# A two-layer decoder on eight cores: instruction order planned for transposes that land late, half of the second layer's weights cast while loading, casts and weight loads in smaller rows

## The chip, the cores and the metric

The program runs on the 8 cores of one Trainium2 chip, each core on one sequence of the batch. A core has five engines that follow their own instruction lists and meet through semaphores: TensorE (PE, matrix products into PSUM), VectorE (DVE), ScalarE (ACT), GpSimd (POOL) and SyncE (SP, which here only issues DMAs). POOL issues DMAs too; those are the only ones that change the number type on the way. The time is device microseconds of the slowest core.

## The reference

```python
x = _mlstm_layer(x, ...)                   # layer A
kv = einsum("bsd,de->bse", x, kv_w)        # shared keys and values
x = _stick_breaking_layer(x, k, v, ...)    # layer B

# layer A
u = einsum("bsd,de->bse", x, w_in)         # q,k | v | o | z | gates
qk = silu(causal_depthwise_conv(qk))       # width 4
h = mlstm_chunkwise(q, k, v, i, f)         # 8 heads; state carried from chunk to chunk
h = sigmoid(o) * head_norm(h) * silu(z)
x = layernorm(ALPHA * x + h @ w_out)
# layer B, 16 heads
q, z = split(x @ w_in)
A[t,s] = sigmoid(z_ts) * prod_{s<j<t}(1 - sigmoid(z_tj)), s < t
x = layernorm(ALPHA * x + (A @ v * silu(z)) @ w_out)
```

Width 2048, sequence 2048, all in float32 outside; the kernel multiplies in bfloat16.

## The kernel before

**How the program is made.** Each part of the work is a generator ("stream") that yields `Op` objects and conditions. `Sched.run` takes, again and again, the stream whose next operation could start earliest by a model of the engines, and records it. So the model decides in which order each engine's list stands; at run time each engine follows its list strictly and waits where an operand is not there. `KB.est` gives the start: the engine's own time, and for each operand the modelled end of its last writer and readers. For a DMA, `KB.dma` models one shared transfer clock `tdma`, to which each transfer adds its `cost`, and says that all it reads and writes is free 1.2 us after that (L157). This holds for what a DMA reads as well: its source may be overwritten only then.

**Layer A, head by head** (8 heads, 32 weight tiles w of two halves u):

- `aload` (L388) has POOL load each weight half from `a_wu` in float32 into RW as bfloat16, 512 KB per DMA; RW holds three w. `wsum` (L439) makes sums and differences of quarters of w, five operations of 1024 columns (L449), three on DVE and two on POOL. They are the stationary operands of a Strassen-like product of `grp` (L586): seven products of eight matmuls each (L604), 56 matmuls for each of 60 groups, 3360 in all; `st["slot"]` counts its steps, seven per group, some 420 in all. `gev` (L614) takes them out of PSUM with ACT (L622) and DVE (L637, L650, L664).
- `conv` (L698) does the convolution and SiLU of q and k for a stretch tb of 512 positions; its last step is on POOL (L723). For k, SP then issues a transpose from KTa (in REGX) to KN (in REGH): "REGH<-REGX". `vtr` (L732) transposes v from VTa (REGH) to VN (REGW): "REGW<-REGH".
- The recurrence has 16 blocks of 128 positions per head, written (head, block). `knw` scales KN on ACT (L779), `recf` is the first matmul of a block (L790, with the mask on DVE at L793), `recm` the others (L804, L806, L810) and the state (DVE L818, ACT L823). `reco` normalises: DVE L836 to L846, POOL L844, and ACT L849, which frees the PSUM bank that L790 of the second block after it writes. The result is transposed by SP ("REGW<-REGW", `hbt`), multiplied by the gates on DVE (L865, `htg`) and stored in `mida`.
- The first block of each stretch tb, that is, blocks 0, 4, 8 and 12 of a head, is the first that needs the new KN and VN.
- `prologue` (L476) computes the gates of all heads once, with a chain of 34 small DVE operations (L513 to L522) between matmuls L509 and L525, while `plain` (L552) multiplies the first weight tiles.

**Between.** `casts` has POOL turn the output weights of layer A (`wao16`) and all 64 weight tiles of layer B (`wb16`) into bfloat16 in HBM, 160 DMAs of 256 KB each (counted in bfloat16), let go by the slot counter; then `wo16` during layer B. `aout` (L937) is the output product of layer A, with its input loaded by SP from `mida`.

**Layer B, 16 heads.** `loads` (L1084) brings a tile of `wb16` into one of four buffers as soon as the tile four before it has been used. Projections are L1098, scores L1179, sigmoid L1184, the product along keys is a scan on DVE (L1206), differences on POOL (L1232), a transpose by SP ("REGX<-REGW"), and the product with v is L1264.

## Time and profile before

| | before |
|---|---|
| median of 3 runs | 2747.32 us (2732.76 to 2823.26) |
| the profiled execution | 2728.98 us |
| its span, slowest core (core 2) | 2727.7 us; the cores span 2678.0 to 2727.7 us |
| busy share of the span | PE 91%, DVE 64%, POOL 47%, ACT 38% |
| weight tiles loaded to SBUF for layer A | 64 DMAs of 512 KB, 9.1 us to landing (median) |
| casts of tiles of layer B | 128 DMAs of 256 KB, 9.1 and 8.5 us to landing |
| DMA | 359.14 MB in 520191 packets |

Matmuls overlap, so that the sum of their durations says little; a wait of PE shows as idle time before a matmul. PE runs its list in order, and so do the other engines.

### The profile page before, as it was taken

How to read it: one execution, taken by the hardware profiler on the slowest of the kernel's cores; microseconds unless marked ns; L12 is line 12 of the kernel's file. 1: busy time of each engine (PE TensorE's matmuls, PEld its weight loads, DVE VectorE, ACT ScalarE, POOL GpSimd, SP SyncE). 2: the span in 40 equal slices, each digit the busy share in tenths (PEclk: the TensorE clock that was granted, in tenths of full speed). 3: DMA queues.
4: the chain of work that ended last, by engine and by line, in shares of the span. 5: the costliest groups of instructions: out<-in, count | busy, mean ns of one | idle time of the engine just before them, and what ended most of it. 6: DMA issues, size and time to landing. Idle time of an engine off the chain costs nothing.

```text
span 2727.7 us, 37420 instructions; the slowest of 8 cores (2678.0 to 2727.7 us)
## 1 busy us (share of the span) xinstructions
PE 2475.2 (91%) x11811; PEld 1136.8 (42%) x11811; DVE 1733.5 (64%) x2859; ACT 1034.4 (38%) x1877; POOL 1290.4 (47%) x1163
## 2 busy tenths in 40 slices
PE   7788988878889886999989999999999999998997
PEld 3343433333344333444434444444444444443443
DVE  2776666656567666566456666666666666656665
ACT  2444443435354444132333444444344344431111
POOL 2554654545455544243345555455555455533433
PEclk9798989988889898999989999999999999999998
DMA  9476877877878776687445656666765555667851
GB/s 155 79 106 101 128 94 114 95 100 100 109 95 127 114 122 187 228 238 210 120 100 119 124 117 120 119 128 121 121 126 103 112 108 111 136 149 188 257 207 78
DMA packets 520191, 359.14 MB, mean 132 GB/s; under 512 B 454208, under 2 KB 487104, under 8 KB 506560
## 3 DMA queue, kind: packets, MB, share of 16 engines
q1 hardware_dynamic: 492688, 214.06, 37.3%
q0 software_dynamic: 27312, 142.69, 29.7%
q8 instruction: 101, 1.65, 0.3%
q14 instruction: 90, 0.74, 0.1%
HBM read 289.60 MB, written 100.66 MB: 143 GB/s over the span
## 4 chain that ended last, share of the span: by engine, by line
PE 59%; DMA 16%; DVE 10%; SPq 6%; issue 4%; POOL 3%; ACT 2%; another core or an unknown queue 0%; DVEq 0%; ACTq 0%; POOLq 0%
PE PSA L1098 23%; PE PSA L937 15%; PE PSA L604 11%; DMA REGH<-REGX 9%; DVE REGW L1206 6%; SPq L160 5%; PE PSA L1264 4%; PE PSA L1179 3%; DMA REGX<-REGW 2%; PE PSA L552 1%; DMA REGW<-REGW 1%; DMA REGX<-x_t 1%; POOL REGW L1232 1%; DMA REGW<-a_wu 1%; DMA mida<-REGW 1%
## 5 line engine op out<-in xcount | busy, mean ns | idle before, releaser
L1098 PE MATMUL PSA<-REGH,REGX 128*128 128x512 bf16 x4096 | 976.3, 380 | 5.9 <-DVE REGW L1105 5.9
L1206 DVE TENSOR_TENSOR_SCAN REGW<-PSA,REGW 128x512 f32<-128x512 f32 (+3 forms) x640 | 684.9, 1091 | 299.4 <-ACT PSA L1184 231.1
L1232 POOL TENSOR_TENSOR REGW<-REGW 128x1024 bf16<-128x1024 f32 (+7 forms) x384 | 527.2, 1391 | 358.2 <-DMA REGX<-REGW 185.2
L1098 PEld LDWEIGHTS PSA<-REGH,REGX 128*128 128x128 bf16 x4096 | 397.5, 98 | 462.2 <-issue 10.4
L1184 ACT ACTIVATE PSA<-PSA 128x512 f32<-128x512 f32 (+3 forms) x640 | 326.8, 519 | 304.2 <-PE PSA L1179 298.8
L604 PE MATMUL PSA<-REGH,REGW 128*128 128x512 bf16 x1680 | 424.7, 394 | 0.0
L604 PE MATMUL PSA<-REGX,REGW 128*128 128x512 bf16 x1680 | 414.8, 388 | 4.1 <-DVE REGW L650 3.0
L604 PEld LDWEIGHTS PSA<-REGH,REGW 128*128 128x128 bf16 x1680 | 167.6, 101 | 183.6 <-issue 22.7
L1110 ACT CAST REGW<-PSA 128x512 bf16<-128x512 f32 x192 | 112.7, 587 | 346.5 <-PE PSA L1098 344.1
L604 PEld LDWEIGHTS PSA<-REGX,REGW 128*128 128x128 bf16 x1680 | 164.8, 100 | 184.6 <-issue 15.8
L937 PE MATMUL PSA<-REGX,REGW 128*128 128x512 bf16 x1024 | 223.5, 382 | 18.6 <-DMA REGW<-mida 18.6
L1179 PE MATMUL PSA<-REGW 128*128 128x512 bf16 (+3 forms) x640 | 220.5, 349 | 15.4 <-DVE REGW L1206 14.8
L937 PE MATMUL PSA<-REGH,REGX 128*128 128x512 bf16 x1024 | 224.0, 381 | 3.6 <-DVE REGW L940 2.6
L844 POOL TENSOR_TENSOR REGW<-REGW,SM 128x1 f32<-128x1 f32 x128 | 81.5, 637 | 227.6 <-DVE REGW L842 207.2
L723 POOL TENSOR_TENSOR REGX<-REGW 128x512 bf16<-128x512 f32 x64 | 86.2, 1347 | 175.3 <-ACT REGW L721 148.0
L937 PEld LDWEIGHTS PSA<-REGX,REGW 128*128 128x128 bf16 x1024 | 100.7, 98 | 141.4 <-issue 22.1
L937 PEld LDWEIGHTS PSA<-REGH,REGX 128*128 128x128 bf16 x1024 | 100.3, 98 | 125.6 <-issue 6.9
L960 ACT ACTIVATE REGW<-REGW,BMVB 128x2048 f32<-128x2048 f32 x26 | 54.4, 2094 | 245.2 <-DVE BMVB L954 245.2
L1264 PE MATMUL PSA<-REGX,REGW 128*128 128x512 bf16 (+3 forms) x640 | 130.1, 350 | 14.4 <-DMA REGX<-REGW 13.2
L160 POOL DMA_DIRECT2D REGX<-wb x64 | 35.8, 559 | 217.9 <-PE PSA L1179 165.3
L449 POOL TENSOR_TENSOR REGW<-REGW 128x1024 bf16<-128x1024 bf16 x60 | 130.5, 2180 | 10.7 <-DVE REGW L449 10.5
L717 DVE SCALAR_TENSOR_TENSOR PSA<-REGW,PRT,PSA 128x512 f32<-128x512 f32 x128 | 96.0, 750 | 53.2 <-ACT PSA L711 52.3
(142 smaller groups left out, 2518.6 us busy)
## 6 DMA issues: line engine op xcount, KB each, us to landing
REGW<-a_wu POOLq DMA_DIRECT2D x64, 512.0 KB, 9.1
REGX<-wb POOLq DMA_DIRECT2D x64, 512.0 KB, 4.6
y<-REGW SPq DMA_DIRECT2D x26, 1024.0 KB, 4.2
wb<-kv_w POOLq DMA_DIRECT2D x64, 256.0 KB, 9.1
wb<-b_w_in POOLq DMA_DIRECT2D x64, 256.0 KB, 8.5
REGW<-y SPq DMA_DIRECT2D x14, 1024.0 KB, 6.8
REGW<-x SPq DMA_DIRECT2D x13, 1024.0 KB, 6.8
wao<-a_w_out POOLq DMA_DIRECT2D x32, 256.0 KB, 6.3
```

Source lines behind the costliest of these rows:

```text
L160: self.eng[q].dma_start(out=out, in_=in_, **kw).then_inc(ent[0], 16)
L449: yield Op(e, lambda: E.tensor_tensor(out=out[0], in0=i0[0], in1=i1[0], op=op), R=i0[1] + i1[1], W=out[1], cost=x)
L604: yield Op("pe", lambda: P_.matmul(PS[bank], lhsT=wo[0][:, c, :], rhs=xo[0][:, c, :], start=(k == 0 and c == 0), stop=(c == 7), skip_group ...
L717: yield Op("dve", lambda: V.scalar_tensor_tensor(out=pc if k else acc, in0=U[u][:, k:k + 512], scalar=wk(k), in1=pc, op0=ALU.mult, op1=ALU ...
L937: yield Op("pe", lambda: P_.matmul(PS[bank], lhsT=mg(c), rhs=wo[:, c, :], start=(c == 0), stop=(c == KC - 1)), R=mgk + wok, W=[("ps", bank ...
L1098: yield Op("pe", lambda c=c: P_.matmul(PS[bank], lhsT=WS[i % 4][:, c, :], rhs=X1[tb][:, c, :], start=(c == 0), stop=(c == KC - 1)), R=[f"W ...
L1110: yield Op("act", lambda: A_.copy(out=dstT[:, tsl], in_=PS[bank]), R=[("ps", bank)], W=[key], cost=0.6, first=True)
L1179: yield Op("pe", lambda: P_.matmul(PS[bank][:, 0:w], lhsT=QTs[par][:, (n - 1) * 128:n * 128], rhs=KTs[par][:, b0 * 128:b1 * 128], start=Tr ...
L1184: yield Op("act", lambda: A_.activation(out=PS[bank][:, 0:w], in_=PS[bank][:, 0:w], func=AF.Sigmoid, scale=-scale), R=[("ps", bank)], W=[( ...
L1206: yield Op("dve", lambda: V.tensor_tensor_scan(out=RR[slot][:, lo:hi][:, ::-1], data0=PS[bank][:, 0:w][:, ::-1], data1=mk[:, ::-1], initia ...
L1232: yield Op("pool", lambda: G.tensor_tensor(out=AA[:, (pos + b0) * 128:(pos + b1) * 128], in0=RR[slot][:, lo + 1:hi + 1], in1=RR[slot][:, l ...
L1264: yield Op("pe", lambda: P_.matmul(PS[bank][:, f0:512], lhsT=VVs[par][:, sb_, :], rhs=TT[:, gp + sb_, f0:512], start=(sb_ == 0), stop=(sb_ ...
```

## The change

1. `KB.dma` has a new argument `lat`, and the transposes to KN, VN and HT are given `lat=LATE`, 14 us in place of 1.2. The transposes of layer B and those between the layers keep 1.2. This changes nothing but the planner's model, and by it the order of the lists.
2. Weight halves of layer A are loaded in two DMAs each, 1024 columns instead of 2048: 128 DMAs of 256 KB instead of 64 of 512 KB.
3. Only the tiles of the first 8 heads of layer B are cast beforehand (64 DMAs instead of 128; with `wao16`, 96 instead of 160). They are let go every 4.0 slots instead of every 2.45. The other 32 tiles are loaded in float32 straight from the inputs and cast by that DMA; the planner counts 4.0 for it instead of 1.5.
4. Casts have another shape. Before, a cast was 16 rows of 8192 elements in HBM; now it is 2x32x2048 (`wao16`, `wo16`) or 2x128x512 (`wb16`), with the 2 outermost.

```diff
+LATE = 14.0
+PRE = 8
...
-    def dma(self, q, slot, out, in_, R=(), W=(), A=(), cost=4.0, **kw):
+    def dma(self, q, slot, out, in_, R=(), W=(), A=(), cost=4.0, lat=1.2, **kw):
...
-        self._time(self.tdma + 1.2, R, W)
+        self._time(self.tdma + lat, R, W)
...
-                yield Op("pool", None, W=rwk[s][2 * u:2 * u + 2], cost=3.0,
-                         dma=dict(slot=f"wu{s}{u}", out=RW[s][:, u].rearrange("p a b -> p (a b)"), in_=a_wu[w, u]))
+                for f in range(2):
+                    yield Op("pool", None, W=[rwk[s][2 * u + f]], cost=1.5,
+                             dma=dict(slot=f"wu{s}{u}{f}", out=RW[s][:, u, 8 * f:8 * f + 8].rearrange("p a b -> p (a b)"),
+                                      in_=a_wu[w, u, :, 1024 * f:1024 * f + 1024]))
...
-            for h in range(NH_B):
+                    for k in range(0, KC, 8):
+                        ca.append((wao16[nb, p:p + 32, k:k + 8], a_w_out[nb, p:p + 32, k:k + 8]))
+                        co.append((wo16[nb, p:p + 32, k:k + 8], b_w_out[nb, p:p + 32, k:k + 8]))
+            for h in range(PRE):
                 for i, (w, u) in enumerate(((kv_w, h), (b_w_in, h), (kv_w, 16 + h), (b_w_in, 16 + h))):
-                    cb += halves(wb16[4 * h + i].rearrange("p (c n) -> p c n", c=KC), w[u], 64)
+                    o = wb16[4 * h + i].rearrange("p (c n) -> p c n", c=KC)
+                    for k in range(0, KC, 8):
+                        cb.append((o[:, k:k + 8], w[u][:, k:k + 8]))
+            fine = lambda x: x.rearrange("p (a b) n -> a p b n", b=4)
             for i, (out, in_) in enumerate(ca + cb):
-                yield lambda: at("slot") >= 10 + 2.45 * i
-                yield Op("pool", None, cost=1.5, dma=dict(slot="casta" if i < len(ca) else "cast", out=out, in_=in_))
+                yield lambda: at("slot") >= 10 + 4.0 * i
+                yield Op("pool", None, cost=1.5, dma=dict(slot="casta" if i < len(ca) else "cast", out=fine(out), in_=fine(in_)))
...
                              dma=dict(slot=f"kn{tb}", out=KN[:, 4 * tb:4 * tb + 4, :],
-                                      in_=KTa[:, tb * 512:(tb + 1) * 512], transpose=True))
+                                      in_=KTa[:, tb * 512:(tb + 1) * 512], transpose=True, lat=LATE))
...
-                yield Op("pool", None, R=["CAST"], W=[f"WB{i % 4}"], cost=1.5,
-                         dma=dict(slot=f"wb{i % 4}", out=WSA[:, i % 4, :], in_=wb16[i]))
+                src, r = (wb16[i], ["CAST"]) if i < 4 * PRE else \
+                    ((b_w_in if i % 2 else kv_w)[(i % 4 // 2) * 16 + i // 4].rearrange("p c n -> p (c n)"), [])
+                yield Op("pool", None, R=r, W=[f"WB{i % 4}"], cost=1.5 if r else 4.0,
+                         dma=dict(slot=f"wb{i % 4}", out=WSA[:, i % 4, :], in_=src))
```

**How the order moves.** Lines below L500 are 7 higher after the change (L604 is L611, L790 is L797, L804 is L811).

First PE's list in head 3 around block (3, 12), the first that needs the keys of the last stretch. Before; the second L804 row is that block:

```order
L804 MATMUL PSA<-REGW 128x257
L604 MATMUL PSA<-REGX,REGW 128x512 x3
L806 MATMUL PSA<-REGW 128x257
L810 MATMUL PSA<-REGW,REGX 128x257
L604 MATMUL PSA<-REGX,REGW 128x512 x2
L604 MATMUL PSA<-REGH,REGW 128x512 x15
L790 MATMUL PSA<-REGX 128x128
L604 MATMUL PSA<-REGH,REGW 128x512
L604 MATMUL PSA<-REGX,REGW 128x512 x14
L790 MATMUL PSA<-REGX 128x128
L604 MATMUL PSA<-REGX,REGW 128x512 x2
L604 MATMUL PSA<-REGH,REGW 128x512 x8
```

After; the second L811 row is block (3, 12):

```order
L811 MATMUL PSA<-REGW 128x257
L611 MATMUL PSA<-REGH,REGW 128x512 x3
L813 MATMUL PSA<-REGW 128x257
L817 MATMUL PSA<-REGW,REGX 128x257
L611 MATMUL PSA<-REGH,REGW 128x512 x2
L611 MATMUL PSA<-REGX,REGW 128x512 x7
L797 MATMUL PSA<-REGX 128x128
L611 MATMUL PSA<-REGX,REGW 128x512
L611 MATMUL PSA<-REGH,REGW 128x512
L811 MATMUL PSA<-REGW 128x257
```

The block before it has moved as well, so that the pieces look alike; what moved is where they stand in the whole. Block (3, 12) had 1518 of the 3360 matmuls L604 ahead of it and now has 1585, and the transpose of its keys, which was recorded when 1483 stood, is recorded when 1438 stand: 35 matmuls between the two before, 147 now.

Next PE's list in the prologue, from the matmuls whose result DVE's chain reads (L509, now L516) to those that need its end (L525, now L532). Before:

```order
L507 MATMUL PSA<-ID,SM 1x128
L509 MATMUL PSA<-REGW,ONE 1x128
L552 MATMUL PSA<-REGH,REGW 128x512 x32
L604 MATMUL PSA<-REGX,REGW 128x512 x8
L525 MATMUL PSA<-REGW,ONE 128x128 x2
```

After:

```order
L514 MATMUL PSA<-ID,SM 1x128
L516 MATMUL PSA<-REGW,ONE 1x128
L559 MATMUL PSA<-REGH,REGW 128x512 x5
L532 MATMUL PSA<-REGW,ONE 128x128 x2
L559 MATMUL PSA<-REGH,REGW 128x512 x20
```

Between the two stood 40 large matmuls, and now stand 5.

Last the end of layer A's projections on PE, up to the output product (L937, now L944). Before:

```order
L804 MATMUL PSA<-REGW 128x257
L604 MATMUL PSA<-REGH,REGW 128x512 x3
L806 MATMUL PSA<-REGW 128x257
L810 MATMUL PSA<-REGW,REGX 128x257
L604 MATMUL PSA<-REGH,REGW 128x512 x20
L937 MATMUL PSA<-REGX,REGW 128x512 x1024
```

After:

```order
L611 MATMUL PSA<-REGH,REGW 128x512 x6
L797 MATMUL PSA<-REGX 128x128
L811 MATMUL PSA<-REGW 128x257
L813 MATMUL PSA<-REGW 128x257
L817 MATMUL PSA<-REGW,REGX 128x257
L797 MATMUL PSA<-REGX 128x128
L811 MATMUL PSA<-REGW 128x257
L813 MATMUL PSA<-REGW 128x257
L817 MATMUL PSA<-REGW,REGX 128x257
L797 MATMUL PSA<-REGX 128x128
L811 MATMUL PSA<-REGW 128x257
```

The last three blocks of head 7 now stand behind the last L611, with nothing between them.

## Rows read from the trace of the kernel before

**Rows 1.** The page's head.
```profile
span 2727.7 us, 37420 instructions; the slowest of 8 cores (2678.0 to 2727.7 us)
```
**Rows 2.** Sums by stage: stretch, length, busy PE, PEld, DVE, ACT, POOL, PEclk, DMA, GB/s.
```profile
95.00:1091.00 996.00, 825.37 (x3887) 383.79 (x3886) 666.88 (x1662) 451.92 (x896) 512.56 (x576) 0.91 0.75 111
1091.00:1314.00 223.00, 223.00 (x1024) 100.64 (x1023) 130.03 (x185) 55.63 (x29) 73.49 (x33) 0.99 0.72 223
1314.00:2467.00 1153.00, 1123.74 (x5335) 515.35 (x5334) 745.42 (x760) 459.23 (x883) 570.21 (x472) 0.99 0.60 119
2467.00:2727.00 260.00, 232.83 (x1069) 104.44 (x1066) 160.08 (x216) 43.05 (x36) 96.69 (x44) 0.97 0.55 182
```
**Rows 3.** PE's longest waits: who waited for whom, us in total, times, longest.
```profile
PE PSA L804 <- ACT REGW L779: 73.8, 15, 14.8
PE PSA L790 <- ACT REGW L849: 42.7, 8, 11.6
PE PSA L937 <- DMA REGW<-mida: 18.6, 1, 18.6
PE PSA L790 <- ACT REGW L709: 5.4, 1, 5.4
```
**Rows 4.** Timeline of PE in head 3: start, duration, instruction, [idle before it, releaser].
```profile
561.55 0.37 PE L804 MATMUL PSA<-REGW 128*128 128x257 bf16 x1 [14.83 <-ACT REGW L779]
...
563.00 1.91 PE L604 MATMUL PSA<-REGH,REGW 128*128 128x512 bf16 x4
564.71 0.42 PE L804 MATMUL PSA<-REGW 128*128 128x257 bf16 x1
...
566.81 2.97 PE L604 MATMUL PSA<-REGX,REGW 128*128 128x512 bf16 x13
...
581.39 12.25 PE L604 MATMUL PSA<-REGX,REGW 128*128 128x512 bf16 x56
593.48 1.89 PE L604 MATMUL PSA<-REGH,REGW 128*128 128x512 bf16 x8
```
**Rows 5.** The second kind of stall: all waits of ACT L779; ACT and PE's timelines.
```profile
ACT REGW L779 <- DMA REGH<-REGX: 153.4, 25, 15.3
...
520.53 0.40 ACT L779 ACTIVATE REGW<-REGH,REGW 128x128 bf16<-128x128 bf16 x1 [13.74 <-DMA REGH<-REGX]
...
522.02 0.27 PE L790 MATMUL PSA<-REGX 128*128 128x128 bf16 x1 [11.59 <-ACT REGW L849]
```
**Rows 6.** DMA issues: tiles, queue, count, size where given, median us to landing.
```profile
REGW<-a_wu POOLq DMA_DIRECT2D x64, 512.0 KB, 9.1
REGX<-wb POOLq DMA_DIRECT2D x64, 512.0 KB, 4.6
...
REGW<-REGH SPq DMA_TRANSPOSE x64, 9.2
...
REGH<-REGX SPq DMA_TRANSPOSE x32, 7.6
```
**Rows 7.** Timeline of PE and of DVE in the prologue.
```profile
91.33 7.43 PE L552 MATMUL PSA<-REGH,REGW 128*128 128x512 bf16 x32
...
100.42 0.71 PE L525 MATMUL PSA<-REGW,ONE 1*128 1x128 f32 x4
...
91.44 0.41 DVE L513 COPY REGW<-PSA 1x256 f32<-1x256 f32 x1 [1.33 <-PE PSA L509]
...
99.59 0.28 DVE L522 TENSOR_TENSOR REGW<-REGW 1x128 f32<-1x128 f32 x1
```
**Rows 8.** Timeline of PE at the end of layer A's projections.
```profile
1067.69 4.48 PE L604 MATMUL PSA<-REGH,REGW 128*128 128x512 bf16 x20
1090.80 9.43 PE L937 MATMUL PSA<-REGX,REGW 128*128 128x512 bf16 x32 [18.63 <-DMA REGW<-mida]
```
**Rows 9.** DVE's waits for weights of layer A.
```profile
DVE REGW L449 <- DMA REGW<-a_wu: 18.4, 6, 4.9
```
**Rows 10.** The software queue, POOL's: packets, MB, share of 16 engines.
```profile
q0 software_dynamic: 27312, 142.69, 29.7%
```

More of the change, by code:

```diff
@@ L455, in casts @@
         def casts():
-            halves = lambda o, i, n: [(o[k * n:(k + 1) * n], i[k * n:(k + 1) * n]) for k in range(2)]
             ca, cb, co = [], [], []
@@ L459, in casts @@
                 for p in range(0, 128, 32):
-                    ca += halves(wao16[nb, p:p + 32], a_w_out[nb, p:p + 32], 16)
-                    co += halves(wo16[nb, p:p + 32], b_w_out[nb, p:p + 32], 16)
-            for h in range(NH_B):
+                    for k in range(0, KC, 8):
+                        ca.append((wao16[nb, p:p + 32, k:k + 8], a_w_out[nb, p:p + 32, k:k + 8]))
+                        co.append((wo16[nb, p:p + 32, k:k + 8], b_w_out[nb, p:p + 32, k:k + 8]))
+            for h in range(PRE):
                 for i, (w, u) in enumerate(((kv_w, h), (b_w_in, h), (kv_w, 16 + h), (b_w_in, 16 + h))):
-                    cb += halves(wb16[4 * h + i].rearrange("p (c n) -> p c n", c=KC), w[u], 64)
+                    o = wb16[4 * h + i].rearrange("p (c n) -> p c n", c=KC)
+                    for k in range(0, KC, 8):
+                        cb.append((o[:, k:k + 8], w[u][:, k:k + 8]))
+            fine = lambda x: x.rearrange("p (a b) n -> a p b n", b=4)
             for i, (out, in_) in enumerate(ca + cb):
-                yield lambda: at("slot") >= 10 + 2.45 * i
-                yield Op("pool", None, cost=1.5, dma=dict(slot="casta" if i < len(ca) else "cast", out=out, in_=in_))
+                yield lambda: at("slot") >= 10 + 4.0 * i
+                yield Op("pool", None, cost=1.5, dma=dict(slot="casta" if i < len(ca) else "cast", out=fine(out), in_=fine(in_)))
             kb.lastw["CASTA"] = [("d_casta", 16 * len(ca))]
@@ L472, in casts @@
                 yield lambda: at("pk") >= 8 + i
-                yield Op("pool", None, cost=1.5, dma=dict(slot="casto", out=out, in_=in_))
+                yield Op("pool", None, cost=1.5, dma=dict(slot="casto", out=fine(out), in_=fine(in_)))
             kb.lastw["CASTO"] = [("d_casto", 16 * len(co))]
@@ L739, in vtr @@
                              dma=dict(slot=f"vn{tb}{u}", out=VN[:, 4 * tb:4 * tb + 4, u * 128:(u + 1) * 128],
-                                      in_=VTa[:, tb % 2, u, :], transpose=True))
+                                      in_=VTa[:, tb % 2, u, :], transpose=True, lat=LATE))
                     vfree[tb % 2, u] = True
@@ L856, in hbt @@
                 yield Op("sp", None, R=[("HB", i % 4)], W=[("HT", i % NHT)], cost=0.6,
-                         dma=dict(slot=f"ht{i % NHT}", out=HT[i % NHT], in_=HB[i % 4], transpose=True))
+                         dma=dict(slot=f"ht{i % NHT}", out=HT[i % NHT], in_=HB[i % 4], transpose=True, lat=LATE))
                 st["hbt"] = i
```

## The prediction
> **What bounds the kernel now.** I read the sums by stage first. The span is 2727.7 us [rows 1], and PE fills nearly all of it except in one stretch: from 95 to 1091 us, the heads of layer A, PE is busy 825 of 996 us, while between the layers it is busy all the time and in layer B's heads 1124 of 1153 us [rows 2]. So 171 us of idle PE lie in layer A, and the granted clock is lowest there too (0.91 on average). Nothing else is full in that stretch: DVE is busy 667 us, POOL 513, ACT 452.
>
> The waits of PE say what ends this idle time. Two kinds are most of it [rows 3]: L804 waits for ACT L779, 73.8 us in 15 times, and L790 waits for ACT L849, 42.7 us in 8 times; one more wait of L790 takes 5.4 us. Both kinds have one cause. L779 reads the transposed keys KN, and ACT waited for that transpose 25 times, 153.4 us in all [rows 5]. The 11.59 us of L790 at 522 us began the same way: ACT stood at L779 until 520.53, 13.74 us, with L849 behind it in its list. By their places in PE's list these stalls all stand within a block or so of the first block of a stretch (0, 4, 8 or 12), where the new keys are first needed.
>
> The order explains it. In the 28 stretches of heads 1 to 7, between 20 and 65 matmuls L604 are recorded between the issue of the key transpose and the first L804 that needs it. A matmul L604 takes 0.216 us (56 of them from 581.39 to 593.48 [rows 4]), so this is 4.3 to 14 us, mostly around 8. The transposes land 7.6 and 9.2 us after issue in the median [rows 6], half of them later. The list thus lets PE arrive too early about every second time.
>
> **The change part by part.**
>
> *Landing at 14 us.* In the built list of after, 79 to 147 matmuls L611 stand between the issue of the key transpose and its first reader in the same 28 stretches, 17 to 32 us. The smallest gain of any is 9.7 us of matmuls; at block (3, 12), which has the longest stall, 14.8 us, it is 24 us (35 matmuls before, 147 now). The transposes themselves are not recorded later: for stretches 2 and 3 mostly earlier. The work that hides the landing is the projection of the next groups, which has to be done anyhow. So of 73.8 + 42.7 + 5.4 = 121.9 us I take away 115 and leave 7 for landings over 17 us: **-115**. Bounds: nothing, if the waits only move, and -122.
>
> *Clock.* Behind the stall that ends at 561.55 us four matmuls L604 take 1.71 us (563.00 to 564.71), 0.43 each, the lower of the two levels (1.2 GHz); at 566.81 they are back at 0.22, 2.4 GHz [rows 4]. So 5.3 us ran at half rate and cost about 2.6 us. PE had idled nearly 15 us before. About 16 stalls of over 4 us belong to the sum above; shorter ones are followed by less. I take 1.5 us each, **-24**, between 0 and -42.
>
> *End of layer A.* PE now waits 18.6 us for the load from mida [rows 8]. In SP's new list the first of these loads stands ahead of the last transposes and no longer behind them. In exchange the last three blocks of the recurrence have no matmul between them; two neighbouring L804 with little between them are 3.2 us apart (561.55 and 564.71), so three take about 10 us, and I leave 4 us for the load: -18.6 + 14 = **-5**, between -9 and +10.
>
> *Prologue.* DVE's chain takes 8.4 us, from 91.44 to 99.87 [rows 7]. It was covered by 40 matmuls of 0.216 us, 8.6 us. Now 5 stand there, 1.1 us, so PE waits 7 us for its end: **+7**. Why it was planned so: the sources of the late transposes count as held too, and so L559 seemed to wait for them.
>
> *Weights of layer A.* Here a cover shrinks. From the last DMA of a weight tile to the first L449 on DVE that reads it, 32 to 96 matmuls were recorded for the tiles from w = 5 on; now it is 20 to 26 for the 14 odd tiles, 41 for every second even one and 86 for the others. 22 matmuls are 4.8 us and 26 are 5.6. A load lands 9.1 us after issue in the median [rows 6], although behind a whole 512 KB each; the last of four DMAs of 256 KB starts behind the other three of its tile. The nearest row for one such DMA is the load of `wb` with 4.6 us: it reads the same 512 KB. So DVE waits between 0 (4.8 of cover against 4.6) and 4 to 5 us (against 9.1) per odd tile. Today DVE waits 18.4 us in 6 times [rows 9] and PE hardly notices. I take 2 us on 14 tiles, two thirds of it passed on to PE, **+18**; bounds 0 and the rival below.
>
> *Casts and issues.* 64 casts fewer and 64 weight DMAs more: POOL issues as many DMAs as before and is only half busy, so nothing. With 64 casts of 256 KB gone from this stage, and with the rest in smaller pieces, transposes should land earlier, which only adds to a cover that is already long; nothing again. The row shows 27312 packets of the software queue with 142.69 MB, 5.2 KB each on average [rows 10], beside transposes in small packets. The Trainium skill (DMA: Bandwidth & Descriptors, Queues, rings and completion order) says that an engine changes between queues only at the end of a packet. By that rule smaller rows would let transposes in sooner; no number above uses it.
>
> *Layer B.* 32 loads read 1 MB instead of 512 KB. A load of bfloat16 lands in 4.6 us, one that casts 512 KB in 9.1 us [rows 6]. Each tile is asked for when the tile four before it is done, about three tiles of 18 us ahead (1153 us for 64 tiles), so either is hidden: 50 us of cover against 9. The lists of PE are the same for the first seven heads and differ by up to 20 matmuls later. **+3** for transposes that meet larger loads, between 0 and +15.
>
> Sum against the profiled execution, 2729 us (2727.7 us of span and 1.3 around it): 2729 - 115 - 24 - 5 + 7 + 18 + 3 = **2613 us**. The median of the runs shown is 18 us above the profiled execution, the lowest 4 above. I add 5: **2618 us**. The cores should also come closer together, since their spans differ by 50 us mostly in these stalls.
>
> **Rivals.**
>
> *The weights take the place of the keys* (chance 0.12). DVE stops at L453 in the 14 odd tiles for 5 us instead of 2, with the subtractions and the state update that PE needs every few matmuls behind it. PE then loses 14 x 5 = 70 us, and about 1.5 us of clock each: 91 instead of 18, 2618 + 73 = 2691. For it speaks the median of 9.1 us against 4.8 of cover; against it that fewer casts lie in the queue.
>
> *The casts spread over two engines only* (0.13). Their outermost dimension is now 2. The software queue moved 142.69 MB in 29.7% of the span, 810 us [rows 10], 1.5 us for a cast of 0.26 MB on all 16 engines; on two it would be 12 us. A slot lasts 2.4 us (996 us over 420), so a cast starts every 9.5 us, and a weight load finds one or two engines with up to 12 us of casts ahead of it. Its tile would land some 6 us later, on 14 tiles with short cover and half that on 7 more: 14 x 6 + 7 x 3 = 105 us of DVE. PE would lose some 80 instead of 18, and 18 of clock: 2698. The Trainium skill (same page, Why a DMA increments its semaphore by 16 and not by 1) has such a rule: the number of engines is the largest up to 16 that divides the slowest dimension. No row here shows a transfer of that shape. What it would do to the transposes is mild, since 14 engines stay free of casts.
>
> *Transposes land much later than 17 us or the recurrence falls behind for another reason* (0.08): half of the 139 us comes back, 2688.
>
> *Slower* (0.04): layer B's casting loads hold up the transposes to TT, on which L1273 waits. DMA engines are busy 0.60 there [rows 2], PE idles only 29 us. To outweigh the gain, each of 32 loads must cost PE over 3.5 us; at 5 us each the time is 2618 + 160 = 2778. Loads of the same kind in layer A, at 0.75, cost PE nothing that the waits show.
>
> **How the numbers follow.** My forecast has 0.63. Two percent, about what a measurement here can tell from no change, is 55 us, a time of 2692. Forecast: all faster. First and second rival: about half each. Third: half. So faster 0.63 + 0.06 + 0.06 + 0.05 = 0.80, the same 0.16, slower 0.04. The likeliest case alone spans 2575 (all bounds on the good side: 2729 - 122 - 42 - 9 + 7 + 0 + 0, plus 5, gives 2568) to 2650. The range up to 2695 takes in most of the rivals and leaves out some 0.15.
>
> **What would show it.** In the new profile the waits of PE at L811 for L786 and at L797 for L856 should be under 15 us together, the clock of the stretch of layer A at 0.96 or more, PE's wait before L944 under 10 us, one wait of about 7 us before L532, and DVE's waits for a_wu 20 to 50 us. The first L944 should start near 970 us. I am wrong if DVE's waits for a_wu are over 70 us with PE waiting for DVE L825, L644 or L657, or if PE gains less than 50 us before its first L944, or if L1273 waits for REGX<-REGW for more than 30 us.

## The result: 3496 us, slower by 27%, and the profile after

| | before | changed |
|---|---|---|
| time, median of 3 runs (us) | 2747.3 | 3496.0 |
| lowest and highest | 2732.8 to 2823.3 | 3471.7 to 3694.2 |
| ratio, 95% interval | 1 | 1.2715 [1.2475, 1.2954] |

The prediction was wrong by its sign: 2618 us was forecast, in a range of 2572 to 2695, and "slower" had a chance of 0.04. In some executions, of either kernel, the cores of one die run at a lower clock; the ratios here and below leave these out, the medians don't.

The profile page of the changed kernel, its head and parts 1 to 4 in extracts:

```profile
span 3494.4 us, 37297 instructions; the slowest of 8 cores (3448.6 to 3494.4 us)
...
PE 2588.9 (74%) x11579; PEld 1163.8 (33%) x11811; DVE 1748.3 (50%) x2859; ACT 1033.8 (30%) x1877; POOL 1336.9 (38%) x1163
...
PE   6676765645545565478997978888667689999897
...
PEclk9788887877777788789998989899888899999999
DMA  9699996637357365387974587978998966787662
...
DMA packets 689151, 342.94 MB, mean 98 GB/s; under 512 B 597568, under 2 KB 646848, under 8 KB 678592
...
q1 hardware_dynamic: 492688, 214.06, 46.8%
q0 software_dynamic: 196272, 126.49, 27.3%
...
PE 38%; issue 26%; DMA 16%; POOL 9%; DVE 7%; SPq 2%; ACT 1%; another core or an unknown queue 0%; POOLq 0%; DVEq 0%; ACTq 0%
```

The work is the same (every engine's busy time is near that of before), but all engines stand idle more. The digits of PE say where: slices 2 to 18 (layer A) and 24 to 32 (layer B's first part) are the poor ones. Also note the software queue. It has 196272 packets where [rows 10] has 27312, with less data. Sums by stretch (length, busy PE, PEld, DVE, ACT, POOL, PEclk, DMA share, GB/s), to set against [rows 2]:

```profile
400.00:1600.00 1200.00, 678.00 (x2824) 298.17 (x2880) 483.70 (x1184) 328.04 (x660) 410.98 (x421) 0.78 0.64 59
1600.00:1800.00 200.00, 193.82 (x875) 87.89 (x893) 124.66 (x194) 52.95 (x31) 70.45 (x32) 0.97 0.83 244
...
2000.00:2800.00 800.00, 600.82 (x2600) 265.59 (x2650) 370.24 (x375) 228.71 (x444) 294.50 (x251) 0.87 0.89 85
2800.00:3200.00 400.00, 388.28 (x1819) 179.48 (x1857) 260.60 (x264) 156.08 (x304) 197.48 (x157) 0.99 0.70 119
```

The poor stretches are those in which casts run: the casts of layer A's and B's weights run up to 1535 us, those of `wo` from 2005 to 2782 us. From 2800 us on PE is busy 388 of 400 us, although the loads that cast directly (2477 to 3154 us) run there. So the casts are suspect, and the direct loads are not. The waits, with who stood, who released it, us in all, times, longest:

```profile
POOL wb L162 <- issue: 656.3, 60, 17.8
...
DVE REGW L853 <- POOL REGW L851: 500.4, 68, 26.3
ACT REGW L856 <- DVE REGW L853: 429.1, 47, 26.2
...
PE PSA L797 <- ACT REGW L856: 367.2, 39, 24.6
```

Read from the bottom: PE waits for ACT, ACT for DVE, DVE for L851 on POOL (GpSimd), and POOL stands 60 times, 656 us in all, ahead of a cast to `wb`, for nothing that the profile shows ("issue"). The timeline shows one such turn (start, duration, instruction, idle before it):

```profile
704.33 1.08 POOL L162 DMA_DIRECT2D wb<-kv_w  x1 [13.22 <-issue]
...
706.47 0.57 POOL L851 TENSOR_TENSOR REGW<-REGW,SM 128x1 f32<-128x1 f32 x1
...
719.47 1.16 POOL L162 DMA_DIRECT2D wb<-kv_w  x1 [12.43 <-issue]
733.64 1.06 POOL L162 DMA_DIRECT2D wb<-b_w_in  x1 [13.00 <-issue]
...
737.12 0.56 POOL L851 TENSOR_TENSOR REGW<-REGW,SM 128x1 f32<-128x1 f32 x1
737.71 0.21 DVE L853 TENSOR_SCALAR REGW<-REGW 128x1 f32<-128x1 f32 x1 [26.14 <-POOL REGW L851]
...
738.07 0.56 ACT L856 ACTIVATE REGW<-PSA,REGW 128x256 bf16<-128x256 f32 x1 [25.95 <-DVE REGW L853]
...
738.78 0.27 PE L797 MATMUL PSA<-REGX 128*128 128x128 bf16 x1 [24.45 <-ACT REGW L856]
```

Between the small L851 at 706.47 and the next at 737.12 stand two casts with 25.43 us of stand, and all four engines wait them out. The casts follow each other after 15.1 and 14.2 us. The issues of DMAs (median us to landing) give the same time for a cast, against 9.1 for `wb<-kv_w` of the kernel before; answering [rows 6]:

```profile
REGW<-a_wu POOLq DMA_DIRECT2D x128, 256.0 KB, 8.8
...
wao<-a_w_out POOLq DMA_DIRECT2D x32, 256.0 KB, 23.1
...
wb<-kv_w POOLq DMA_DIRECT2D x32, 256.0 KB, 15.4
...
wo<-b_w_out POOLq DMA_DIRECT2D x32, 256.0 KB, 15.2
...
REGW<-REGH SPq DMA_TRANSPOSE x64, 10.9
...
REGH<-REGX SPq DMA_TRANSPOSE x32, 9.6
```

So each cast waits until the one ahead of it has landed, and POOL, which executes in order, waits with it. Worked out from the trace for all 64 casts to `wb`: 59 of them begin within 0.5 us of the landing of the cast ahead (0.3 us in the median), and they begin 16.6 us apart on average. The 32 casts to `wao` before them don't wait so: they begin 11.3 us apart and land after 23.1 us, so two or more are under way at a time.

### The profile page after: what moved, and what is told of

It reads as the page before. It is cut to its first block, busy times and chain, and to the rows that moved or that the text cites. A ratio compares the mean times of both kernels' runs of the same rounds, so it can differ in the third digit from the quotient of the medians.

```text
span 3494.4 us, 37297 instructions; the slowest of 8 cores (3448.6 to 3494.4 us)
## 1 busy us (share of the span) xinstructions
PE 2588.9 (74%) x11579; PEld 1163.8 (33%) x11811; DVE 1748.3 (50%) x2859; ACT 1033.8 (30%) x1877; POOL 1336.9 (38%) x1163
## 2 busy tenths in 40 slices
DMA packets 689151, 342.94 MB, mean 98 GB/s; under 512 B 597568, under 2 KB 646848, under 8 KB 678592
## 3 DMA queue, kind: packets, MB, share of 16 engines
q0 software_dynamic: 196272, 126.49, 27.3%
## 4 chain that ended last, share of the span: by engine, by line
PE 38%; issue 26%; DMA 16%; POOL 9%; DVE 7%; SPq 2%; ACT 1%; another core or an unknown queue 0%; POOLq 0%; DVEq 0%; ACTq 0%
PE PSA L1107 14%; PE PSA L944 12%; DMA REGX<-REGW 10%; PE PSA L611 5%; PE PSA L1273 3%; DVE REGW L1215 3%; POOL REGW L1241 3%; DMA REGH<-REGX 2%; SPq L162 2%; DMA REGW<-REGW 2%; PE PSA L1188 2%; PE PSA L559 1%; POOL REGX L730 1%; POOL REGW L851 1%; POOL wb L162 1%
## 5 line engine op out<-in xcount | busy, mean ns | idle before, releaser
L1241 POOL TENSOR_TENSOR REGW<-REGW 128x1024 bf16<-128x1024 f32 (+7 forms) x384 | 527.1, 1390 | 595.4 <-DMA REGX<-REGW 355.9
L1107 PEld LDWEIGHTS PSA<-REGH,REGX 128*128 128x128 bf16 x4096 | 403.5, 99 | 477.4 <-issue 39.0
L611 PE MATMUL PSA<-REGX,REGW 128*128 128x512 bf16 x1641 | 444.2, 409 | 86.9 <-DVE REGW L657 59.5
L611 PE MATMUL PSA<-REGH,REGW 128*128 128x512 bf16 x1642 | 458.2, 419 | 64.6 <-ACT PSA L629 51.3
L797 PE MATMUL PSA<-REGX 128*128 128x128 bf16 x128 | 30.2, 236 | 397.6 <-ACT REGW L856 367.2
L853 DVE TENSOR_SCALAR REGW<-REGW 128x1 f32<-128x1 f32 x128 | 26.9, 210 | 501.8 <-POOL REGW L851 500.4
L611 PEld LDWEIGHTS PSA<-REGH,REGW 128*128 128x128 bf16 x1680 | 176.1, 106 | 271.8 <-issue 126.4
L611 PEld LDWEIGHTS PSA<-REGX,REGW 128*128 128x128 bf16 x1680 | 170.8, 104 | 283.8 <-issue 133.5
L944 PE MATMUL PSA<-REGH,REGX 128*128 128x512 bf16 x1004 | 222.8, 381 | 5.3 <-DVE REGW L947 3.4
L944 PE MATMUL PSA<-REGX,REGW 128*128 128x512 bf16 x1004 | 222.3, 382 | 1.1
L1273 PE MATMUL PSA<-REGX,REGW 128*128 128x512 bf16 (+3 forms) x634 | 147.2, 384 | 79.9 <-DMA REGX<-REGW 78.7
L856 ACT ACTIVATE REGW<-PSA,REGW 128x256 bf16<-128x256 f32 x128 | 71.8, 561 | 450.4 <-DVE REGW L853 429.1
L162 POOL DMA_DIRECT2D wb<-kv_w x32 | 36.0, 1125 | 335.0 <-issue 331.8
L162 POOL DMA_DIRECT2D wb<-b_w_in x32 | 36.0, 1125 | 326.0 <-issue 324.5
L797 PEld LDWEIGHTS PSA<-REGX 128*128 128x128 bf16 x128 | 13.1, 102 | 428.9 <-issue 420.8
L1188 PEld LDWEIGHTS PSA<-REGW 128*128 128x128 bf16 x640 | 63.8, 100 | 242.4 <-issue 179.5
## 6 DMA issues: line engine op xcount, KB each, us to landing
wao<-a_w_out POOLq DMA_DIRECT2D x32, 256.0 KB, 23.1
```

Source lines behind the costliest of these rows:

```text
L162: self.eng[q].dma_start(out=out, in_=in_, **kw).then_inc(ent[0], 16)
L611: yield Op("pe", lambda: P_.matmul(PS[bank], lhsT=wo[0][:, c, :], rhs=xo[0][:, c, :], start=(k == 0 and c == 0), stop=(c == 7), skip_group ...
L856: yield Op("act", lambda: A_.activation(out=HB[i % 4], in_=PS[b][:, 0:256], func=AF.Identity, bias=s(1), scale=s(3)), R=[("ps", b), sk(1), ...
L944: yield Op("pe", lambda: P_.matmul(PS[bank], lhsT=mg(c), rhs=wo[:, c, :], start=(c == 0), stop=(c == KC - 1)), R=mgk + wok, W=[("ps", bank ...
L1107: yield Op("pe", lambda c=c: P_.matmul(PS[bank], lhsT=WS[i % 4][:, c, :], rhs=X1[tb][:, c, :], start=(c == 0), stop=(c == KC - 1)), R=[f"W ...
L1188: yield Op("pe", lambda: P_.matmul(PS[bank][:, 0:w], lhsT=QTs[par][:, (n - 1) * 128:n * 128], rhs=KTs[par][:, b0 * 128:b1 * 128], start=Tr ...
```

## The experiments

Theory A: the new shape of the casts is what costs (A1: because its outermost axis has two rows, so that two DMA engines do all of a cast; A2: because it has many small packets), and the order planned for late transposes is worth what was forecast. Theory B: the new order is what fails on the chip. Theory C: the direct loads. Each ratio is against runs of the kernel before on the same chip.

Two kinds of transposes are told apart below, as in [rows 6]: "REGH<-REGX", 32 times, brings the keys to KN, and "REGW<-REGH", 64 times, brings the values to VN. The text ahead of e11 calls the second kind "key transposes"; its 22.2 us are those of the values.

### The shape of the casts, in the changed kernel

**e1_old_casts.** Only the shape is put back:

```diff
...
-                        cb.append((o[:, k:k + 8], w[u][:, k:k + 8]))
...
+                    cb += halves(wb16[4 * h + i].rearrange("p (c n) -> p c n", c=KC), w[u], 64)
...
-                yield Op("pool", None, cost=1.5, dma=dict(slot="casto", out=fine(out), in_=fine(in_)))
+                yield Op("pool", None, cost=1.5, dma=dict(slot="casto", out=out, in_=in_))
```

> The changed kernel with its casts in the shape of before (16 partitions of 8192 elements, 64 partitions of 2048), still one for each 4.0 slots and still for half of layer B's units; order, split weight loads and direct loads stay as changed. Theory A (the new shape of the casts stops GpSimd): the stand of about 11 to 13 us before each cast of a unit disappears, casts land in 8 to 10 us instead of 15.4, L853's wait for GpSimd's L851 (500 us in the changed kernel) falls under 100 us, and the time is 2600 to 2690. Theory B (the order planned for late transposes is what is fragile on the chip): the casts land sooner but the time stays over 3000. Theory C (the fewer casts and direct loads): over 2900, with the excess in layer B.

Measured: 2618.3 us, 0.9595 [0.953, 0.966] of before. The stand ahead of the casts is gone (0.5 us in all, once). PE's longest waits for other engines, and the landing of the transposes:

```profile
PE PSA L794 <- ACT REGW L853: 21.7, 7, 5.7
...
PE PSA L810 <- DVE REGW L797: 15.7, 10, 3.2
```

```profile
REGW<-REGH SPq DMA_TRANSPOSE x64, 6.7
...
REGH<-REGX SPq DMA_TRANSPOSE x32, 3.7
```

`wb` casts land in 7.3 us. B and C fall: all of the loss of 27% hangs on the shape.

**e6_no_fine.** Column halves of all rows, but no second split of a row:

```diff
-            fine = lambda x: x.rearrange("p (a b) n -> a p b n", b=4)
+            fine = lambda x: x
```

> The changed kernel without the reordering of the casts' axes: a cast of a unit is 128 partitions of one row of 1024 elements (256 KB written, as before), a cast of the output weights 32 partitions of 4096. Theory A1 (the outermost axis of two puts a cast on two of the 16 DMA engines): with 128 or 32 outermost the packets (1024 or 4096 elements, 2048 or 8192 B) run on 16 engines, a cast lands in 8 to 10 us, GpSimd does not stand, time 2600 to 2700. Theory A2 (the number of small packets is what costs, wherever they run): half as many packets of twice the size take half of the excess away, a stand of about 6 us before a cast and about 3050. Theory B (the order): still about 3450.

Measured: 2613.7 us, 0.9575 [0.9521, 0.9628], casts of `wb` land in 8.0 us. By A2 half of the loss would have stayed; none did.

**e7_rows_outermost.** As many packets and as small, with the partitions outermost:

```diff
...
-            fine = lambda x: x.rearrange("p (a b) n -> a p b n", b=4)
+            fine = lambda x, j: x.rearrange("p (a c b) n -> p a c b n", a=2, c=2)[:, :, j]
...
```

> The changed kernel with casts of the same number and size of packets (256 of 512 elements for a unit, 64 of 2048 for the output weights), but with the 128 (or 32) partitions as the outermost axis and the two pieces of a row inside it (chunks 0 to 3 and 8 to 11 of a row, then 4 to 7 and 12 to 15, so that they do not merge). Theory A1 (two outermost rows, two engines): the packets spread over 16 engines, landing 8 to 10 us, stand before a cast under 3 us, time 2600 to 2720. Theory A2 (the number and size of packets): landing near 15 us and time near 3450, as in the changed kernel.

Measured: 0.9545 [0.9461, 0.9628], the profiled execution 2606.0 us, casts of `wb` land in 9.0 us (8.3 for `b_w_in`). A2 falls: 256 packets of 1024 B cost nothing that can be measured if the partitions are outermost. The profile page's line on packets of this kernel says one thing more:

```profile
DMA packets 545791, 342.37 MB, mean 131 GB/s; under 512 B 454208, under 2 KB 503488, under 8 KB 535232
```

The changed kernel has 689151 - 545791 = 143360 packets more, and its packets under 512 B are 597568 - 454208 = 143360 more, so every extra packet is tiny (in the trace they have 4 B). The number fits one count exactly: in the changed kernel a cast of a `wb` unit has 256 rows and thus 128 on each of two engines, one to `wao` or `wo` 64 and thus 32. If each of the other 14 engines gets as many 4-byte packets ("dummies") as each of the two gets rows, 64 x 14 x 128 + 64 x 14 x 32 = 143360. Beside it, at 650 to 750 us mostly two packets of 1024 B (98 ns each) are under way at a time while a cast runs, and 256 x 98 ns / 2 = 12.5 us. That is most of a cast's 15 us. The Trainium skill (DMA: Bandwidth & Descriptors, Why a DMA increments its semaphore by 16 and not by 1) has the number of engines as the largest up to 16 that divides the slowest dimension of both sides. The trace agrees, with two.

**e8_two_outermost.** Few large packets, and two outermost. The casts are those of e1, taken in pairs of partitions:

```diff
...
+            two = lambda x: x.rearrange("(p a) ... -> a p ...", a=2)
...
-                yield Op("pool", None, cost=1.5, dma=dict(slot="casto", out=out, in_=in_))
+                yield Op("pool", None, cost=1.5, dma=dict(slot="casto", out=two(out), in_=two(in_)))
```

> The changed kernel with casts of the old regions, but their partitions taken as (pairs, 2) with the pair index outermost: 2 outermost, 32 inside, rows of 2048 elements for a unit (2, 8 and 8192 for the output weights), so few large packets (64 and 16) and yet two outermost. Theory A1 with GpSimd held by the transfer as such: landing still about 15 us, GpSimd stands about 11 us before each cast, time near 3450. Theory R (what holds GpSimd is room for descriptors: 256 of them fill it, 64 do not): landing 13 to 16 us, since two engines still move 256 KB, but no stand before the next cast, and a time of 2620 to 2720. Theory A2 (number of packets): landing 8 to 9 us and 2600 to 2690.

Measured: 3152.3 us, 1.1528 [1.1429, 1.1628]. The packets under 512 B are 490048 - 454208 = 35840 above e1, which is 64 x 14 x 32 + 64 x 14 x 8: two engines again, by the same count. None of the three expectations holds whole. POOL's stand is as theory R has it:

```profile
POOL wb L162 <- issue: 38.9, 4, 12.4
```

But the time R gave, 2620 to 2720, is missed by 430 us. With POOL free to issue, the other transfers are late:

```profile
REGW<-a_wu POOLq DMA_DIRECT2D x128, 256.0 KB, 15.7
...
REGW<-REGW SPq DMA_TRANSPOSE x192, 9.0
...
REGW<-REGH SPq DMA_TRANSPOSE x64, 22.2
...
REGH<-REGX SPq DMA_TRANSPOSE x32, 10.3
```

```profile
DVE REGW L870 <- DMA REGW<-REGW: 142.9, 19, 16.1
...
DVE REGW L453 <- DMA REGW<-a_wu: 96.9, 20, 22.7
...
ACT REGW L784 <- DMA REGH<-REGX: 71.6, 10, 21.9
```

The transposes of the values land after 22.2 us instead of 6.7 (e1), those of the keys after 10.3 instead of 3.7, those of the results (`hbt`) after 9.0 instead of 3.9, and the weights after 15.7 instead of 6.8. No engine's wait is put down to the values, for all that they land last. The engines wait for the results, the weights and the keys (1.4, 33.3 and 21.5 us in e1). So there are two harms: casts on two engines each, and POOL's stand.

The casts in flight don't share one pair of engines. Worked out from the traces while the casts to `wb` run: in e8 four to ten of their packets of 4096 B are under way at once in 30% of the time, and none in 32%; in e11 below, where the casts run one by one, it is two in 65% and more than four never. So no pair was simply full in e8. What is seen is that the others' packets take longer: a transpose's packet of 256 B takes 113 ns on average in e8's heads of layer A and 39 ns in e1's. By what way a cast on two engines delays them isn't shown.

**e11_ring_quarter.** e8 with less room for descriptors:

```diff
-    nc = bass.Bass("TRN2", target_bir_lowering=False, dynamic_dma_scratch_size=4096)
+    nc = bass.Bass("TRN2", target_bir_lowering=False, dynamic_dma_scratch_size=1024)
```

Measured: a span of 3499.3 us (three executions, 3500.8 the lowest), and

```profile
POOL wb L162 <- issue: 602.8, 55, 16.1
```

```profile
REGW<-REGH SPq DMA_TRANSPOSE x64, 10.9
```

The stand is back, with the packets of e8 (566271 of them in both), and the transposes of the values land in 10.9 us, as in the changed kernel (those of the keys in 11.7, against 9.6 there). Theory R holds by all its numbers: 128 descriptors per engine at 4096 fill what 32 per engine fill at 1024. Since nothing but the room was changed against e8, that room is what POOL waits for. Doubling it in the changed kernel, which would be the other half of this proof, wasn't run. Whether the fullest engine counts or the sum over all 16, dummies included, can't be told: both are four times as large for a cast to `wb` in the changed kernel as here.

**e2_before_fine.** Is the new order needed for the harm? The kernel before, with the new shape alone (the diff of e1 the other way round, all 16 heads):

> The kernel before with only the changed kernel's shape of casts, in all 128 casts of units and 64 of output weights, still one for each 2.45 slots. Theory A1 (two outermost rows put each cast on two engines): each cast of a unit takes about 15 us and GpSimd stands for it, 128 x 15.5 = 1984 us against the 960 us of casts in the kernel before: 3600 to 4200 us, with the same sign in the rows (a stand of 11 to 13 us before each cast). If the shape needs the new order to do harm: under 3000.

Measured: one execution of 4148.0 us, a granted clock of 0.81, and POOL's stand

```profile
POOL wb L160 <- issue: 1344.3, 121, 18.4
```

The shape alone does it. The changed kernel has half as many casts of units, and POOL's stand is half as long.

### The other parts, one by one

**e3_before_late.** The kernel before, with the order planned for late transposes and nothing else:

```diff
+LATE = 14.0
...
-        self._time(self.tdma + 1.2, R, W)
+        self._time(self.tdma + lat, R, W)
...
-                         dma=dict(slot=f"ht{i % NHT}", out=HT[i % NHT], in_=HB[i % 4], transpose=True))
+                         dma=dict(slot=f"ht{i % NHT}", out=HT[i % NHT], in_=HB[i % 4], transpose=True, lat=LATE))
```

> The kernel before with only the planned landing of the transposes put 14.0 behind the transfer (keys, values and the activations' transposes), casts, weight loads and the second layer untouched. The prediction's steps landing (-115), clock (-24), end of layer A (-5) and prologue (+7) all hang on this order: about 140 us under the kernel before, so 2580 to 2610; L811's and L797's waits for the transposes (there L810, L796 or near) under 15 us together. Rival (the fewer casts are what lets the transposes land in time): under 60 us of gain here, and the waits shrink only by half.

Measured: 2647.8 us, 0.9657 [0.9561, 0.9753], so 0.034 x 2739 = 94 us. The waits of PE answering [rows 3] in this kernel's profiled core:

```profile
PE PSA L791 <- ACT REGW L850: 89.9, 9, 24.9
PE PSA L553 <- DMA REGX<-x_t: 17.4, 5, 12.8
...
PE PSA L805 <- ACT REGW L780: 4.5, 3, 2.7
```

L805's wait (73.8 us before) is nearly gone, but the other kind is not: 89.9 us on this core, the slowest, and 15.2 to 58.5 on the other seven. ACT stands for transposes here 44.2 us at L780 (keys, 31.6 the longest) and 60.6 us at L850 (results, 26.0 the longest): with 128 casts of `wb` in the old shape some still land later than 14 us. The gain was two thirds of what was expected here, and above the rival's 60 us.

**e4_before_pre8.** The kernel before with half of layer B's units cast by their loads; 64 casts fewer, 4.0 slots apart:

```diff
+PRE = 8
...
-            for h in range(NH_B):
+            for h in range(PRE):
...
-                yield lambda: at("slot") >= 10 + 2.45 * i
+                yield lambda: at("slot") >= 10 + 4.0 * i
...
```

> The kernel before with only layer B's heads 8 to 15 cast by their loads, and so 64 casts fewer, spaced 4.0 slots apart, in the old shape. By the prediction's steps (casts 0, layer B +3): within 5 us of the kernel before. Rival (half the casts were in the transposes' way): the transposes land sooner (8 us instead of 9.2) and 20 to 60 us are gained in layer A.

Measured: 2666.1 us, 0.9725 [0.9651, 0.9799], so 75 us gained, without any change of the order. The rival is right, and by more than its 20 to 60 us:

```profile
wb<-kv_w POOLq DMA_DIRECT2D x32, 256.0 KB, 5.5
...
REGW<-REGH SPq DMA_TRANSPOSE x64, 3.2
...
REGH<-REGX SPq DMA_TRANSPOSE x32, 5.8
```

The transposes of the values land in 3.2 us instead of 9.2, those of the keys in 5.8 instead of 7.6 [rows 6].

**e5_before_split.** The kernel before with each weight load in two halves:

```diff
+                for f in range(2):
+                    yield Op("pool", None, W=[rwk[s][2 * u + f]], cost=1.5,
...
```

> The kernel before with only layer A's weight loads split into halves of 1024 columns. The prediction's step weights (+18) was made for the new order, where a slot is shorter; in the old order the loads have more cover, so 0 to +18 us; each half lands in 6 to 9 us. Rival (finer loads let DVE's casts start earlier): -5 to -15 us.

Measured: 2734.4 us in the profiled execution and 2735.3 in one more, against 2724.2 to 2738.8 of before. Two executions are too few for an interval; no difference is seen, so neither the 18 us of the prediction nor the rival's gain can be told from nothing here.

**e10_late_pre_unsplit.** e1 without that split, so the order, half of the casts and the direct loads:

```diff
-                for f in range(2):
-                    yield Op("pool", None, W=[rwk[s][2 * u + f]], cost=1.5,
...
+                yield Op("pool", None, W=rwk[s][2 * u:2 * u + 2], cost=3.0,
...
```

> The changed kernel with casts in the old shape and with whole weight loads too (so: order, half of the casts, direct loads). Against the same kernel with split loads (2618, 0.9595 of before) this tells the price of the split in the new order. By the prediction's step weights (+18) it is about 2600, ratio 0.953; if the split costs nothing, 2618 again; if the split is what shortens the waits for weights, 2630 or more.

Measured: 2589.6 us, 0.9458 [0.9381, 0.9536]. Against e1 the split costs 0.0137 x 2739 = 38 us, twice the 18 of the prediction; the intervals just meet, and the runs were on two chips, so the size is rough. DVE waits for these weights 33.3 us in 13 times in e1 and 18.2 in 10 here.

**e15_pre4 and e16_pre1.** e10 with fewer units cast ahead, the first with 4 heads (below), the second with PRE = 1 and 9.6 slots:

```diff
-PRE = 8
+PRE = 4
...
-                yield lambda: at("slot") >= 10 + 4.0 * i
+                yield lambda: at("slot") >= 10 + 6.0 * i
```

> The combination of the order, old casts, whole weight loads and direct loads of half of the units (2590, 0.9458 of before), with only a quarter of the units cast ahead (heads 0 to 3) and casts 6.0 slots apart. Fewer casts lay 72 us in the kernel before, where transposes were waited for; with the new order those waits are down to about 20 us: -5 to -15 us in layer A, and +1 to +3 for more direct loads in layer B: 2575 to 2590. Rival (direct loads of 1 MB in 4.0 us each crowd layer B's queue once there are 48 of them): 2600 to 2630 with new waits for wb tiles.

> The same with only head 0 cast ahead (4 units, 8 casts), casts 9.6 slots apart: if casts cost layer A by their traffic, another -5 to -10 us in layer A; if direct loads cost layer B, the loss shows here first, at heads 1 to 3, where the projections wait for units just after the layers' boundary. 2565 to 2600.

Measured: 2570.4 us, 0.9422 [0.9355, 0.9489], and 2585.3 us, 0.9464 [0.9375, 0.9552]. With e10 these are three kernels that can't be told apart: the first half of the casts removed brought 75 us (e4), the rest nothing that is measured. Nor is there a sign of the rival, direct loads that crowd layer B: it takes 1378 us in e15 and 1385 in e16, and 1385 in e10. Any of the three beats both kernels of this case.

### Where the time is, stage by stage

Worked out from the traces: the time of PE's first projection matmul (L604 before), of its first output product of layer A (L937), of the first matmul of layer B's recurrence (L1179), and of the end of the last output product; median of the eight cores, differences in us.

| kernel | to first L604 | heads of A | between | layer B |
|---|---|---|---|---|
| before | 99 | 967 | 237 | 1379 |
| changed | 117 | 1479 | 237 | 1612 |
| e8 (two engines a cast, POOL free) | 116 | 1132 | 238 | 1617 |
| e11 (two engines a cast, POOL stands) | 128 | 1466 | 236 | 1632 |
| e2 (before, new shape) | 98 | 2216 | 237 | 1564 |
| e1 (changed, old casts) | 116 | 844 | 237 | 1383 |
| e3 (order alone) | 111 | 857 | 237 | 1375 |
| e4 (half the casts alone) | 98 | 891 | 237 | 1386 |
| e10 (order, half the casts) | 111 | 815 | 237 | 1385 |

Against e1 the shape costs 635 us in layer A's heads: 288 with casts on two engines each and POOL free (e8), and 334 to 347 more when POOL also stands (e11, changed). In layer B it costs about 230 us, and there e8 and the changed kernel are alike. That is the casts to `wo`, with 32 descriptors or fewer per engine, ahead of which POOL does not stand. While they run, some of the transposes from `REGW` to `REGX` are late (4.0 us in the median of all 256 in the changed kernel and in e1 alike), and L1241 on POOL waits for them. The changed kernel and e1:

```profile
POOL REGW L1241 <- DMA REGX<-REGW: 355.9, 48, 20.0
```

```profile
POOL REGW L1238 <- DMA REGX<-REGW: 184.4, 47, 11.9
```

## Point by point: why the prediction was wrong

**The step that failed is "Casts and issues": nothing.** It cost 878 us: 3496.0 against 2618.3 in e1, 635 of them in the heads of layer A and some 230 in layer B. The step went by the number of issues and by POOL's busy share, and said that smaller pieces could only help the transposes. Both halves fail. POOL is busy 38% and stands 656 us all the same, because an issue can wait for room; a busy share does not show that. And smaller pieces don't help: with casts on two engines the transposes of the values land in 10.9 us against 6.7 in e1, those of the keys in 9.6 against 3.7; with pieces as small on 16 engines (e7) it is 6.6 and 4.1.

**The rival that had the cause had its size wrong, and by that the sign of the whole.** "The casts spread over two engines only" had the rate right: 12 us for a cast, and 13 to 15 were measured where casts run one by one. It let them overlap, and priced a delay of 6 us on single weight tiles, 80 us in all. Its next sentence has a cast starting every 9.5 us; casts of 12 us that run one by one can't keep up with that. In the changed kernel the casts to `wb` do run one by one, since POOL has no room for the next, and begin 16.6 us apart: 492.6 to 1535.4 us, 1043 of the 1479 us of the heads. In e2 they are 14.6 us apart, 1858 of 2216 us. Nothing in the prediction had this wait for room. Where POOL is free the casts do overlap (e8: 10.5 and 12.0 us apart, 20.1 to 24.4 to landing), and 12 against 9.5 doesn't set the length; the 288 us of e8 are the other transfers' delays. The rival called those mild for the transposes because 14 engines stay free; the values landed after 22.2 us and the keys after 10.3. And it left out the `wo` casts of layer B, 230 us.

**Two of its signs of being wrong came.** PE's first L944 begins at 1596 us (117 + 1479, median of the cores) and not near 970. L1273 waits 78.7 us for "REGX<-REGW", where over 30 was to count. This sign was meant for the loads that cast directly, the rival "slower"; but e1 has the same loads and waits 14.3 us there, so it was the casts to `wo`.

**Landing, clock, end of layer A and weights** add up to -115 - 24 - 5 + 18 = -126 us before the first L944, and e1 measures 967 - 844 = -123. But the parts are different from what the sum says. The order alone brings 110 (e3), where landing, clock and end of layer A stood at 144; fewer casts alone 76 (e4), where 0 stood; both together 152 (e10), and the split takes 29 of them back, where 18 stood. So the order was over-sized by some 34 us, fewer casts were under-sized by the 42 that they add to the order, and the weights by 11. That the late transposes of e3 are what the order fell short by is likely, and not shown apart. The misses cancelled. The two kinds of waits that the new order was to end, under 15 us together in the forecast, are 21.7 us in e1, and DVE's waits for weights 33.3 (20 to 50 forecast). PE's first L941 (the changed kernel's L944) begins at 969.0 us in e1 on the slowest core (970 forecast). The clock of its heads is 0.97 (0.96 or more forecast):

```profile
116.00:969.00 853.00, 791.11 (x3787) 374.05 (x3863) 659.93 (x1614) 442.83 (x885) 499.40 (x564) 0.97 0.75 107
```

**End of layer A**: right. The 18.6 us of [rows 8] are gone in e1, where PE goes from the last block to its first L941 without a wait (4 us were left for it). The three blocks before it, from the end of the last L608 at 957.34, take 11.6 us (10 forecast):

```profile
955.88 1.46 PE L608 MATMUL PSA<-REGH,REGW 128*128 128x512 bf16 x5
...
968.74 0.42 PE L814 MATMUL PSA<-REGW,REGX 128*128 128x257 bf16 x1
968.95 6.39 PE L941 MATMUL PSA<-REGX,REGW 128*128 128x512 bf16 x22
```

**Prologue**: right in kind, too small in size. PE's wait before L532 is 7.3 us (7 forecast), but it also waits 10.8 us instead of 5.8 for DVE a few matmuls earlier, and the split adds 5 (e1 against e10): +17 where +7 stood.

**Layer B**: +3 forecast for the direct loads, and +7 measured in e4, +4 in e1. These loads have 128 partitions outermost.

**The sum.** With the casts on 16 engines the time is 2618.3 us in the median, and the sum was 2618. That it agrees to the microsecond is luck, by the misses above.

## What to carry to other kernels

Read a DMA's outermost dimension before its packet size: in this kernel, casts with two rows outermost ran on two engines of 16 each and cost 878 us, and as many bytes in the same small packets with 128 partitions outermost cost nothing that was measured. When a transfer is to be confined to few engines, set its time on these engines beside the time between two such transfers, and ask whether the next can be issued while the last is under way. If it can't, the longer of the two times sets the length of the stage, as here; if it can, look for what the transfers do to all others. And an engine that issues DMAs needs two budgets, its busy time and the descriptors in flight; the second shows as idle time with the releaser "issue" ahead of a DMA.

## What the runs showed that was not expected

- The counts fit dummies of 4 B on the engines that a cast doesn't use: 143360 and 35840 extra packets, exactly 14 x rows per engine for each cast. 128 descriptors per engine at a scratch size of 4096 and 32 at 1024 stop POOL until the cast ahead has landed (656 and 603 us); 32 at 4096 do not (39 us).
- A kernel that throttles itself can look better in its transfers than one that doesn't: with POOL held back the transposes of the values landed in 10.9 us, with POOL free in 22.2, at 3496 and 3152 us. Those of the keys hardly tell the two apart (9.6 and 10.3).
- Casts that run beside transposes cost them more than their share of bytes says: 64 casts fewer (16.8 MB of 359 MB) took the transposes of the values from 9.2 to 3.2 us, those of the keys from 7.6 to 5.8, and 76 us from the stage. What in the casts does it (reads, writes or packets) stays open. e7 shows that it is not the size of the packets.
